# Two modulations at a time: moving the adaLN projections out of the mixers' output products into two feed-forwards

## What is computed

```
for l in range(DEPTH):
    mods = (jax.nn.silu(c) @ w_ada[l] + b_ada[l]).reshape(B, 1, N_MOD, D_MODEL)
    sh, sc, g = mods[:, :, 0], mods[:, :, 1], mods[:, :, 2]
    f = _swiglu(x * (1.0 + sc) + sh, w_ffn_in[l, 0], w_ffn_out[l, 0])
    x = _layernorm(DEEPNORM_ALPHA * x + 0.5 * g * f, ln_g[l, 0], ln_b[l, 0])
    sh, sc, g = mods[:, :, 3], mods[:, :, 4], mods[:, :, 5]
    h = x * (1.0 + sc) + sh
    ...
    x = _layernorm(DEEPNORM_ALPHA * x + g * y, ln_g[l, 1], ln_b[l, 1])
    sh, sc, g = mods[:, :, 6], mods[:, :, 7], mods[:, :, 8]
    f = _swiglu(x * (1.0 + sc) + sh, w_ffn_in[l, 1], w_ffn_out[l, 1])
    x = _layernorm(DEEPNORM_ALPHA * x + 0.5 * g * f, ln_g[l, 2], ln_b[l, 2])
```

## Time and profile before

| | us |
|---|---|
| median of 3 runs | 2702.23 (2700.34 to 2702.49) |
| the profiled execution | 2700.04 |
| its span, first to last instruction | 2698.2 |
| PE busy | 2485.4 (92%) |
| POOL busy | 1093.0 (41%) |
| DVE busy | 898.5 (33%) |
| ACT busy | 846.3 (31%) |
| mean granted TensorE clock | 0.952 |

### The profile page before, as it was taken

One profiled execution on the slowest core, in us unless ns is written; L12 is line 12 of the kernel. 1 busy time (PEld: TensorE's weight loads), 2 busy tenths in 40 slices (PEclk: granted clock), 3 DMA queues, 4 the chain that ended last, 5 costly groups with the idle time before them and its releaser, 6 DMA issues.

```text
span 2698.2 us, 45513 instructions
## 1 busy us (share of the span) xinstructions
PE 2485.4 (92%) x18440; PEld 2228.1 (83%) x18440; DVE 898.5 (33%) x1069; ACT 846.3 (31%) x1176; POOL 1093.0 (41%) x544
## 2 busy tenths in 40 slices
PE   7999999799889988699999989999979886999996
PEld 2899999779843337599999889999979875999995
DVE  1122202446243445622210442220253456222214
ACT  3222333432312234332232342223332244322213
POOL 1344477424400012444457644447653314444433
PEclk9999999989969979899999999999999998999998
DMA  7233354247313325233255323335512361333331
GB/s 266 65 91 93 118 169 143 77 129 224 109 48 106 105 91 174 63 94 93 86 165 153 102 60 91 93 115 164 151 47 79 101 188 56 94 93 93 96 92 48
DMA packets 448321, 298.44 MB, mean 111 GB/s; under 512 B 20102, under 2 KB 422118, under 8 KB 448086
## 3 DMA queue, kind: packets, MB, share of 16 engines
q1 hardware_dynamic: 448214, 296.92, 36.5%
HBM read 291.36 MB, written 5.53 MB: 110 GB/s over the span
## 4 chain that ended last, share of the span: by engine, by line
PE 38%; issue 17%; DVE 6%; POOL 6%; DMA 2%; ACT 2%; SPq 0%; POOLq 0%; ACTq 0%; DVEq 0%
PE ps L709 26%; POOL w_lo L659 5%; PE ps L980 3%; DMA raw<-w_out_even 1%; PE ps L732 1%; PE ps L966 1%; PE ps L970 1%; PE ps L734 1%; DMA raw<-w_out_odd 1%; DVE sq_sum L1604 1%; DVE ada_lo_proj L427 1%; DVE ada_lo_h L427 1%; PE ps L1019 1%; PE ps L1012 1%; DVE rdev L1644 1%
## 5 line engine op out<-in xcount | busy, mean ns | idle before, releaser
L659 POOL TENSOR_TENSOR w_lo<-raw,w_hi 128x1024 fp32r<-128x1024 f32 (+1 forms) x308 | 803.2, 2609 | 1235.4 <-ACT w_hi L1217 1235.1
L709 PE MATMUL ps<-h_hi,w_hi 128*128 128x260 f32 x3584 | 729.3, 285 | 25.0 <-POOL w_lo L659 15.8
L1217 ACT ACTIVATE w_hi<-raw 128x1024 fp32r<-128x1024 f32 (+1 forms) x308 | 346.7, 1127 | 1225.0 <-PE ps L709 1107.8
L709 PE MATMUL ps<-h_hi,w_lo 128*128 128x260 f32 x3584 | 727.8, 285 | 0.0
L709 PE MATMUL ps<-h_lo,w_hi 128*128 128x260 f32 x3584 | 727.2, 285 | 0.0
L709 PEld LDWEIGHTS ps<-h_hi,w_hi 128*128 128x128 f32 x3584 | 559.0, 191 | 30.2 <-POOL w_lo L659 12.6
L709 PEld LDWEIGHTS ps<-h_hi,w_lo 128*128 128x128 f32 x3584 | 558.5, 190 | 0.0
L709 PEld LDWEIGHTS ps<-h_lo,w_hi 128*128 128x128 f32 x3584 | 557.7, 190 | 0.0
L709 PE MATMUL ps<-hid_hi,w_hi 128*128 128x260 f32 x1408 | 284.7, 283 | 0.0
L709 PE MATMUL ps<-hid_hi,w_lo 128*128 128x260 f32 x1408 | 283.9, 283 | 0.0
L709 PE MATMUL ps<-hid_lo,w_hi 128*128 128x260 f32 x1408 | 283.1, 283 | 0.0
(11 more groups left out here) (296 smaller groups left out, 2377.3 us busy)
## 6 DMA issues: line engine op xcount, KB each, us to landing
raw<-w_ffn_in SPq DMA_DIRECT2D x176, 512.0 KB, 3.6
ada_w<-w_ada SPq DMA_DIRECT2D x120, 512.0 KB, 4.3
raw<-w_ffn_out SPq DMA_DIRECT2D x64, 704.0 KB, 4.4
pages<-cache_k SPq DMA_DIRECT2D x64, 256.0 KB, 2.9
pages<-cache_v SPq DMA_DIRECT2D x64, 256.0 KB, 2.9
raw<-w_in_even SPq DMA_DIRECT2D x28, 512.0 KB, 4.2
raw<-w_in_odd SPq DMA_DIRECT2D x24, 512.0 KB, 3.7
ada_first<-w_ada SPq DMA_DIRECT2D x5, 2048.0 KB, 14.0
```

The lines of the kernel that those rows point to most:

```text
L659: pool.tensor_tensor(w_lo[:, k, 0:kt, :], raw[:, k, 0:kt, :], w_hi[:, k, 0:kt, :].bitcast(F32), ALU.subtract).then_inc(chunk_cut, 1)
L709: mm = pe.matmul(ps[:, 2 * q + half, 0:HT], w[:, k, t, :], v[:, kt0 + t, half, :], start=start and t == 0 and step == 0, stop=stop and t = ...
L1217: act.activation(w_hi[:, k, 0:kt, :], raw[:, k, 0:kt, :], ACT.Identity).then_inc(hi_cut, 1)
```

## The change

The table `ADAS` says which modulations a second product makes: that of sub-layer 0 makes those of 1 and 2, that of 2 makes 3, that of 3 makes 4 and 5; the second products of 1, 4 and 5 make none. Where two are made, 48 pieces come with 16 chunks, three to a chunk (`PIECES[2]`), the first inside the product, two behind it. The low parts of slots 0 and 1 are then made by GpSimd, those of slot 2 by VectorE, ahead of the residual. The cut of the next chunk but one moves ahead of the copy of sums that follows the second piece. `mod` holds three modulations instead of two, the turned sums of the second one get other places in the same PSUM banks, and VectorE finishes the second modulation right after the first, behind the normalised tiles; TensorE waits for that before it goes on in the mixer. `ada_cut` becomes one semaphore for each slot. Some small buffers share space.

```
+ADAS = {0: (1, 2), 1: (), 2: (3,), 3: (4, 5), 4: (), 5: ()}
+PIECES = {0: ((), ()), 1: ((0, 1), (2,), (3, 4), (5,)), 2: ((0, 1, 2), (3, 4, 5), (6, 7, 8), (9, 10, 11))}
...
+        def lows_of(eng_is_dve, n, now):
+            return tuple(q for q in now if (len(ADAS[n]) == 2 and q % NADA == 2) == eng_is_dve)
...
             def pieces(n, i, pieces_now):
                 for q in pieces_now:
-                    c = (n - 1) * MT + i * 6 + q
-                    if not (n == 1 and is_first(i) and q < NADA):
-                        sp.wait_ge(ada_cut, c - NADA + 1)
+                    if not (n == 0 and is_first(i) and q < NADA):
+                        sp.wait_ge(ada_cut[q % NADA], cuts_before(n, i, q))
...
-                                if n + 1 < last:
-                                    pieces(n + 1, i, PIECES[2][2 * j + k])
+                                if ADAS[n]:
+                                    pieces(n, i, PIECES[len(ADAS[n])][2 * j + k])
...
                         chunk(chunks_before(n, True) + i * 2 + k, k, mixer_out[n][:, :, bass.ds((i * 2 + k) * 128, 128)], KT)
-                        if n + 1 < last:
-                            pieces(n + 1, i, PIECES[1][k])
...
-                pe.wait_ge(mod_steps, mod_steps_before(EVEN + 1))
+                pe.wait_ge(mod_steps, mod_steps_before(EVEN + 2))
...
-                            product(chunks_before(n, True) + i * 2 + k, k, k, KT, hi, lo,
-                                    between=lambda t: pieces(n + 1, i, now[t // 3 - 1:t // 3]) if t in (3, 6) else None)
+                            product(chunks_before(n, True) + i * 2 + k, k, k, KT, hi, lo)
...
-                    cuts = [((now[-1] if len(now) > 1 else now[-1] + 1) - 0.5, 2, 0)] if chunk else []
+                    cuts = [(now[0] + 0.5, 2, 0)] if chunk else []
...
+            def dve_lows(n, j):
+                return lows_of(True, n, sum(PIECES[len(ADAS[n])][2 * j:2 * j + 2], ()))
...
-                        if n not in FFN and n + 1 < last:
-                            low_pieces(dve, n, i, PIECES[1][j])
+                        low_pieces(dve, n, i, dve_lows(n, j))
                         product_done(i, j)
...
-                    gate(n + 1)
+                    if ADAS[n]:
+                        gate(n + 1)
+                        for m in ADAS[n][1:]:
+                            modulation(m)
+                            gate(m)
```

More of the change, by code:

```diff
@@ L65, in mod_steps_before, with groups_before, pieces_before @@
     return 4 + 7 * (n - 1) if n else 0
+def groups_before(n):
+    return sum(GROUPS * len(ADAS[i]) for i in range(n))
+def pieces_before(n, i=0, q=0):
+    return 2 * groups_before(n) + 6 * len(ADAS[n]) * i + q
 def ffns_before(n):
@@ L210, in build_step @@
         c_parts = new("c_parts", [128, KT, 18], F32R)
-        mod = new("mod", [128, 2, MT, 9])
+        mod = new("mod", [128, 3, MT, 9])
         mod_b = new("mod_b", [128, KT, 9])
@@ L340, in build_step @@
         ada_hi_cut = sem("ada_hi_cut")
-        ada_cut = sem("ada_cut")
+        ada_cut = [sem(f"ada_cut{k}") for k in range(NADA)]
         ada_turned = sem("ada_turned")
@@ L376, in is_first, with turned_at @@
             return isinstance(i, int) and i == 0
+        def turned_at(n, g):
+            second = n in (2, 5)
+            if g < GATE_GROUP:
+                return (7, ADA_W + 72 + g * 18) if second else (6, g * 18)
+            return (6, 144 + (g - GATE_GROUP) * 18) if second else (7, ADA_W + (g - GATE_GROUP) * 18)
         def mixed_tile(t):
@@ L679, in second_body @@
                         def second_body(i):
-                            for u, now in enumerate(PIECES[per_tile]):
+                            for u in range(2 * per_tile):
                                 c = chunks_before(n, True) + i * 2 * per_tile + u
                                 cut(c, u % 2, kt)
-                                if n in FFN and n + 1 < last:
-                                    low_pieces(pool, n, i, now)
+                                if ADAS[n]:
+                                    low_pieces(pool, n, i, lows_of(False, n, PIECES[len(ADAS[n])][u]))
                         loop(pool, False, KT // 2, second_body)
@@ L1114, in first_piece @@
                             pe.wait_ge(gate_done, f0 + FT)
-                        pieces(n + 1, i, now)
+                        pieces(n, i, now)
                     def body(i):
@@ L1121, in body @@
                                     pe.wait_ge(drained, 2 * (KT * n + i * 2 + j - 1))
-                                now = PIECES[2][2 * j + k] if n + 1 < last else ()
+                                now = PIECES[len(ADAS[n])][2 * j + k] if ADAS[n] else ()
                                 if is_first(i) and (j, k) == (0, 1):
@@ L1130, in body @@
                                     shift_sums(n)
-                                pieces(n + 1, i, now[1:])
+                                pieces(n, i, now[1:])
                     second_product(n, body)
@@ L1417, in body @@
                             chunk = (c0 + i * 2 * per_tile + u + 2, u % 2, next_kt if beyond else kt)
-                        if n + 1 == last and chunk:
+                        if not ADAS[n] and chunk:
                             cut(*chunk)
-                        if n + 1 < last:
-                            then = (steps + (tuple(q + 6 for q in steps[0]),))[u + 1]
-                            if static and i == KT // 2 - 1 and then[0] >= 6:
+                        if ADAS[n]:
+                            then = (steps + (tuple(q + per_i for q in steps[0]),))[u + 1]
+                            if static and i == KT // 2 - 1 and then[0] >= per_i:
                                 then = ()
@@ L1619, in residuals @@
                 for t in range(KT // 2, KT):
-                    if n not in FFN and n + 1 < last:
-                        low_pieces(dve, n, t // 2, PIECES[1][t % 2])
-                    if t == MODULATE_AT and n + 1 < last:
+                    low_pieces(dve, n, t // 2, dve_lows(n, t % 2))
+                    if t == MODULATE_AT and ADAS[n]:
                         modulation(n + 1)
```

92 lines of the change are left out of this document (47 added, 45 removed).

## The result

| | before | changed |
|---|---|---|
| median of 4 runs, us | 2702.36 (2700.34 to 2703.74) | 2766.48 (2758.54 to 2768.64) |
| the profiled execution, us | 2700.04 | 2758.54 |
| its span, us | 2698.2 | 2756.7 |
| PE busy, us | 2485.4 | 2511.2 |
| mean granted TensorE clock | 0.952 | 0.937 |

The changed kernel is slower: ratio 1.0229, 95% interval 1.0212 to 1.0246. In a second set of runs beside the experiments it was 1.0221 (1.0185 to 1.0257). The forecast was 2745 us with a range of 2680 to 2774. The sign and the range held. The change was forecast as 43 us; by the medians it is 64.

What follows compares the result with a forecast made beforehand. In feed-forwards 0 and 3 the loop through the third piece's low part, its reload and the chunk's load was the bound: 146.4 us cost, less 103.5 gained in the mixers, is +42.9, so 2745 us, range 2680 to 2774.

Steps and rivals of the forecast that it cites:

- first cut late: Feed-forwards 0 and 3: the first cut comes 2.0 us late, its load standing behind three low parts.
- mixer's projection: Both mixers: projection 49.3 us plus last residual 2.0 late, from 103.8 and 102.3; total gain 103.5 us.
- the loop: Feed-forwards 0 and 3: cut, third piece's low part, its reload, then next chunk's load; 26.6 us per pair against TensorE's 24.2.
- Rivals 2 and 3: Feed-forwards 0 and 3: cheaper loop, pair 24.2, 2686 us, chance 0.15; or TensorE bounds throughout, 2667 us, chance 0.12.
- rival 3: Feed-forwards 0 and 3: TensorE bounds throughout, squares hidden; 33 + 1.4 us each, net -35, 2667 us; chance 0.12.
- The walk's sums: Feed-forwards 0 and 3: step times from cut to next cut, 13.4 us even, 13.2 odd, 15.9 even when cold.
- Rival 1: Feed-forwards 0 and 3: every pair cold at 29.1 us, 82.4 us each, net +61.3, 2763 us; chance 0.18.
- Pair on time: Feed-forwards 0 and 3: two chunks' rounds at full clock, 26.6 us; half of the pairs taken so.
- Late pair: Feed-forwards 0 and 3: turning at half clock, VectorE behind GpSimd's chunk cut, pair 29.1 us; half of the pairs taken so.
- Squares: Second half of feed-forwards 0 and 3: VectorE's squares delay the third piece's low part, 11.0 us (bounds 0 and 17).
- rival 4: Mixers don't speed up: ScalarE waits for VectorE's squares, 16 us more for both, 2761 us; chance 0.06.
- The rest: Second modulation's small VectorE operations, hidden while TensorE waits: nothing, or 2 us each without that cover; feed-forward 2 keeps its order.

Runs made afterwards that it cites:

- The first experiment: Changed kernel, but SyncE issues each chunk's load ahead of the three pieces that stood before it: 2682.53 us, ratio to before 0.9945.
- the kernel with both edits: Changed kernel with each chunk's load ahead of the pieces before it and, in even steps, the copy of sums ahead of the cut: 2670.42 us, ratio 0.9868.
- by experiment: Changed kernel, but in the second half VectorE makes the low part of the next tile's first third piece ahead of this tile's squares: 2735.43 us.
- the one with the sums ahead: Changed kernel, but in every even chunk's step ScalarE copies the second piece's sums ahead of the cut: 2724.73 us, ratio 1.0098.

## Why the prediction was right, and where it was short

FF is feed-forward; the second profile is that of the changed kernel again.

| us | forecast | first profile, FF 0 / FF 3 | second profile, FF 0 / FF 3 |
|---|---|---|---|
| first cut late | 2.0 | 3.4 / 5.9 | 4.2 / 5.9 |
| first half, 4 pairs | 111.6 | 112.9 / 110.4 | 114.6 / 112.9 |
| second half, 3 pairs | 94.7 | 95.9 / 96.1 | 100.4 / 98.6 |
| last even cut to last residual | 12.9 | 14.2 / 14.0 | 14.1 / 13.9 |
| mixer's projection | 51.3 | 52.4 / 51.7 | |

**The bound** was the forecast's: the loop, not TensorE, and cuts released by loads. The first experiment cut one link and the pair fell to 24.26 us, where the prediction had 24.2 for TensorE alone. (Its own terms, 15.84 + 6 x 0.94 + 3 x 0.54 + 0.8, add up to 23.9; with the 0.8 us gap gone the pair was 23.93.) Rivals 2 and 3 (cheap loop, TensorE-bound) did not happen here; rival 3's 2667 us is what the kernel with both edits gives.

**The walk's sums.** Some of them do not come out of their terms. 7.2 + 6.1 is 13.3, not 13.4; 5.9 + 1.0 + 6.1 is 13.0, not 13.2; and with the same landing the cold round is 9.5 + 1.0 + 6.1 = 16.6, not 15.9. The pairs would be 26.3 and 29.6, and their mean of 28.0 is near the 27.9 used. Rival 1's 82.4 likewise comes out as 81.6 from its own terms, and the kernel with all pairs warm as 2727, not 2725.

**Pair on time** (the prediction's warm one). Forecast 26.6, measured 27.3 to 28.1, on the average 27.6. The term that was short is the landing in the even round: from the chunk's load to its cut it is 6.9 us (1929.89 to 1936.80), not 6.1, and 6.8 to 7.6 in all seven such rounds. In the rounds walked the steps up to the load came within 0.4 us.

**Late pair** (the prediction's cold one). Forecast 29.1, measured 27.6 to 29.9, on the average 28.6. The place that VectorE misses came as walked: it ended at +9.3 (forecast 9.5). But the load behind it lands in 5.0 to 5.7 us, so the even round takes 15.3 us, not 15.9. Being late costs 1.0 us per pair and not the 2.5 of the forecast. The mean of the sixteen first-half pairs of both profiles is 28.2, near the 27.9. This is in part luck: one kind was priced 1.0 us too low and the other 0.5 too high, and that half would be late (9 of 16 were) was a choice between two rows.

**Rival 1,** every pair cold at 2763 us, names nearly the measured time, but not by its own reason. It needed every pair at 29.1, and they were 28.2 in the first half; in the second they are 31 to 35, but there the squares take 3 to 5 us of each. The Trainium skill, TensorE: Matmul & The Clock Gate, "HAM oscillation", says of a loop that waits 3 to 5 us for a load in each turn that every turn starts cold. The traces agree in part: here the clock falls in every first-half pair, also after gaps of 1.8 to 2.5 us, which the earlier trace rows had let me think safe. But after these it falls only 1.5 to 1.9 us after TensorE has resumed, when turning and third piece are done or nearly so, and the loop hardly sees it:

```profile
1952.00:1953.50 1.50, 1.50 (x13) 1.30 (x14) 0.00 (x0) 0.87 (x1) 0.56 (x1) 1.00 0.00 0
1953.50:1957.10 3.60, 3.60 (x21) 3.60 (x20) 1.67 (x1) 1.06 (x1) 3.60 (x2) 0.54 0.12 27
1957.10:1964.00 6.90, 6.90 (x58) 6.56 (x57) 0.00 (x0) 1.32 (x2) 4.79 (x2) 0.99 0.79 245
```

That is a pair on time: 3.4 of its 27.7 us are at 1.2 GHz, inside the product, where TensorE has slack.

**The wait of VectorE for GpSimd** set the low part's end in both kinds of round, 1.1 us behind the end of GpSimd's operation. GpSimd pays for it too: its chunk cut took 4.20 us at 1927.95 and 3.21 at 1872.52. The Trainium skill, SBUF — State Buffer, "Who interferes with whom", has these two engines share a port pair under an exclusive lock when VectorE reads both its inputs from SBUF, as here; the traces agree.

**Squares.** Forecast 11.0 per stage, by experiment 13.8 and 10.3 against the first profile.

**Start of the stage.** The most mis-sized term: 2.0 against 3.4 and 5.9. Chunk 2's load went out at 343.02, behind the low parts of three pieces, and was cut 6.2 us later, at 349.27; of that queue I had counted only a part.

**Mixers.** 102.0 us gained, forecast 103.5. Nothing new came up there (rival 4 fell).

**The rest** was put at nothing and is not quite: 0.9 and 1.2 us in the sub-layers behind the mixers, 1.0 and 0.6 for the norm behind the feed-forwards (forecast 1.4), and 2.9 us at start and end of the program. Why these stretches are longer is not shown. The sum is 77.0 + 76.9 + 1.6 - 102.0 + 2.1 + 2.9 = 58.5. Of the 15.6 us over the forecast, 10.3 are in the two stages, three quarters of it at their starts and ends.

## What to carry to other kernels

When a stage feeds two streams of loads from one queue, put the load that sets the pace ahead of those that wait for a buffer: a wait at the head of the queue passes to whatever stands behind it, here 75 us of 2766. Walk the loop link by link with the durations that its neighbours show under contention; that gave each step up to the load within half a microsecond, and the landing, for which there was no row, 0.8 too short. Count the first and the last round apart, since there other loads and the next stage's work stand in the queue.

## What the runs showed that I had not expected

The granted clock fell after gaps of 1.78 to 2.53 us too (0.94 over such a pair, 3.4 us of it at 1.2 GHz), though one gap of 2.20 us before had let it stay.

A stretch that no edit touches differs between executions: at the attention's start the clock stays at 1.2 GHz some 20 us longer in one profile than in another, which is worth 8.7 us from there to the mixer's projection. The changed kernel, then the one with the sums ahead, at the same place of the program:

```profile
874.90:894.90 20.00, 20.00 (x26) 3.66 (x24) 7.10 (x17) 1.78 (x4) 0.00 (x0) 0.50 0.15 45
...
856.80:876.80 20.00, 20.00 (x46) 4.97 (x44) 8.71 (x21) 2.38 (x6) 0.00 (x0) 0.84 0.23 65
```

The runs of before spread from 2689 to 2708 us over the three sets; how much of that is this stretch is not shown. Stages should be compared, not only totals.
